# Attention of the second block: where a short block's shares stand, and the order of the last head pair's blocks

## The reference, cut to what matters

```
scale = 1 / sqrt(dqk)
sc = einsum('bqhd,bkhd->bhqk', q, k) * scale
sc = where(kpos <= qpos, sc, -inf)
o  = einsum('bhqk,bkhd->bqhd', softmax(sc), v)
```

## Time and profile before

| | us |
|---|---|
| median of 3 runs | 3968.17 (3967.4 to 3969.49) |
| the profiled execution | 3971.36 |
| its span | 3969.6 |
| TensorE busy | 3730.8 (94%) |
| VectorE busy | 2176.8 (55%) |
| ScalarE busy | 1226.5 (31%) |
| mean granted TensorE clock | 0.977 of full speed |

### The profile page before, as it was taken

One profiled execution on the slowest core, in us unless ns is written; L12 is line 12 of the kernel. 1 busy time (PEld: TensorE's weight loads), 2 busy tenths in 40 slices (PEclk: granted clock), 3 DMA queues, 4 the chain that ended last, 5 costly groups with the idle time before them and its releaser, 6 DMA issues. The chain is left out here.

```text
span 3969.6 us, 50076 instructions
## 1 busy us (share of the span) xinstructions
PE 3730.8 (94%) x19547; PEld 1925.4 (49%) x19547; DVE 2176.8 (55%) x3611; ACT 1226.5 (31%) x2432; POOL 792.3 (20%) x714
## 2 busy tenths in 40 slices
PE   6999899999899999999999989898999898998898
PEld 3444454454577774444444434344554354554443
DVE  7688426644466666533217767523555444444578
ACT  3333132465355544511110001111231254454400
POOL 0000000000566664411214332223110000000132
PEclk8999999999999999999999999999999999999999
DMA  5122664476655445401325633321111100000233
GB/s 191 48 48 52 114 133 117 113 132 120 159 179 178 170 136 171 163 32 64 117 85 180 212 108 130 106 87 61 48 38 35 34 4 6 8 4 4 72 115 111
DMA packets 594911, 385.36 MB, mean 97 GB/s; under 512 B 414468, under 2 KB 531304, under 8 KB 591988
## 3 DMA queue, kind: packets, MB, share of 16 engines
q1 hardware_dynamic: 577811, 314.52, 28.6%
q0 software_dynamic: 10336, 42.47, 3.0%
q10 hardware_dynamic: 6528, 25.17, 1.6%
HBM read 251.28 MB, written 130.55 MB: 96 GB/s over the span
## 5 line engine op out<-in xcount | busy, mean ns | idle before, releaser
L667 PE MATMUL bank<-uT,front_W 128*128 128x512 f32 (+1 forms) x1216 | 488.2, 563 | 4.7 <-ACT front_b_ L874 4.7
L599 PE MATMUL bank<-uT,front_W 128*128 128x512 f32 (+1 forms) x896 | 363.1, 563 | 0.0
L667 PEld LDWEIGHTS bank<-uT,front_W 128*128 128x128 f32 x1216 | 232.1, 192 | 252.3 <-issue 245.9
L599 PEld LDWEIGHTS bank<-uT,front_W 128*128 128x128 f32 x896 | 169.8, 191 | 182.8 <-issue 179.5
L3446 ACT ACTIVATE attn_pT<-bank 128x512 f32<-128x512 f32 x232 | 122.8, 595 | 195.5 <-PE bank L3386 194.6
L3482 DVE TENSOR_SCALAR_CACHE_REDUCE attn_sc_odd<-bank 128x512 f32<-128x512 f32 (+2 forms) x160 | 91.5, 606 | 167.1 <-PE bank L3376 167.1
L1357 POOL TENSOR_TENSOR scan_U<-scan_U,gla_w 128x512 f32<-128x512 f32 x144 | 146.9, 1041 | 168.4 <-DVE scan_U L1545 168.4
L1768 PE MATMUL bank<-gates_T,gates_S 128*128 128x512 f32 x384 | 172.7, 592 | 1.3 <-POOL uT L1730 1.3
L3373 PE MATMUL bank<-attn_kT,attn_qT 64*128 64x512 f32 (+3 forms) x640 | 151.0, 572 | 8.7 <-DVE attn_sc_odd L3482 6.3
L3398 PE MATMUL bank<-attn_pT,uT 128*64 128x256 f32 (+1 forms) x1152 | 139.2, 376 | 11.9 <-DVE attn_pT L3503 10.0
L1347 POOL TENSOR_TENSOR front_work<-front_work,eGl 128x512 f32<-128x512 f32 x144 | 146.9, 1041 | 10.6 <-DVE front_work L1564 4.3
(11 more groups left out here) (570 smaller groups left out, 7267.2 us busy)
## 6 DMA issues: line engine op xcount, KB each, us to landing
merge_gates<-gates_r ACTq DMA_DIRECT2D x16, 1024.0 KB, 4.0
uT<-merge_gates SPq DMA_DIRECT2D x16, 1024.0 KB, 10.7
gla_asks_keys_values<-front_a SPq DMA_DIRECT2D x14, 1152.0 KB, 10.8
front_W<-in_w_in SPq DMA_DIRECT2D x28, 512.0 KB, 10.6
uT<-in_w_in SPq DMA_DIRECT2D x13, 1024.0 KB, 5.3
scan_dq<-delta_qkv SPq DMA_DIRECT2D x16, 768.0 KB, 6.2
front_work<-gla_asks_keys_values SPq DMA_DIRECT2D x16, 768.0 KB, 7.0
front_work<-delta_qkv SPq DMA_DIRECT2D x16, 768.0 KB, 6.0
```

The lines of the kernel that those rows point to most:

```text
L599: m = pe.matmul(bank[:, conv_bank(f, b), 0:n], W[:, f % 2, k, :], uT[:, k, t0:t0 + n], start=(k == 0), stop=(k == KT - 1))
L667: mm = pe.matmul(bank[:, b, 0:n], W[:, s, k, :], uT[:, k, t0:t0 + n], start=(k == 0), stop=(k == KT - 1))
```

## The change

First, `rest_end(prev)` is called right behind the last group of the block before, if that block has fewer groups than this one has pieces. In pairs 1 to 3 this concerns block (a - 1, 0), whose `H` comes after the first piece and the one group instead of after the fourth piece of (a, 7). Second, the last pair takes its blocks as 7, 6, 3, 4, 1, 0, 5, 2; there the new place of `rest_end` also concerns block 3 under block 4 and block 0 under block 5. Third, the closing loop handles the groups of whatever block is last (two, for p = 2), with the product of the block before it at the first group, and changes bank pairs between groups.

```diff
-        blocks = [(a, p) for a in range(PAIRS) for p in range(TOP, -1, -1)]
+        DOWN, LAST = range(TOP, -1, -1), (7, 6, 3, 4, 1, 0, 5, 2)
+        blocks = [(a, p) for a in range(PAIRS) for p in (DOWN if a < PAIRS - 1 else LAST)]
...
                 if k < of_rest:
                     rest_items(prev, k, k >= pieces(p))
+                    if k == of_rest - 1 and of_rest < pieces(p):
+                        rest_end(prev)
...
-            if prev:
+            if prev and of_rest >= pieces(p):
                 rest_end(prev)
-        for k in range(len(groups(0))):
-            order.append(("O", *blocks[-2]))
+        for k in range(len(groups(blocks[-1][1]))):
+            if k == 0:
+                order.append(("O", *blocks[-2]))
             rest_items(blocks[-1], k, False)
+            pairs_of_banks.reverse()
         rest_end(blocks[-1])
         order.append(("O", *blocks[-1]))
```

## The result

The changed kernel takes 3987.0 us (median of 5) against 3969.5 for the kernel before (5 runs): ratio 1.0043, 95% interval 1.0028 to 1.0057, so 17.5 us slower. A second timing on another occasion gave 3985.9 against 3970.0, ratio 1.0044 (1.0031 to 1.0056). The profiled execution of the changed kernel took 3982.05 us (span 3980.3), 10.7 more than the profiled execution before; its attention is longer by 14.5 us, and it came to attention 3.8 us earlier (first scores at 3143.87 against 3147.66).

The account below looks back on a forecast made before the run. TensorE, busy for 94% of the span, was taken as the bound, with attention's end paid one for one. Moved shares 0.4, waits 9.1 and clock 6.0 sum to 15.5 us over the 3968.17 median, say 3984; range 3974 to 3992.

Parts of the forecast that it names:

- Bound and exposure: Whole kernel: TensorE is busy for 94% of the span, and the end of attention is paid one for one.
- Shares moved: Three head changes: 4.85 us of lateness goes, three delays of 1.69 come, about 0.05 remains each time; net +0.4 us.
- (a): Last pair, block 4 behind block 3: TensorE waits 3.1 us for exponentials that block 1's scores do not cover.
- (b): Last pair, block 5 behind block 0: shares wait 1.13 us, third piece 0.94, and uncovered exponentials 4.0.
- The third piece's wait: Last pair, block 5: its third piece waits 0.94 us for VectorE's evictions.
- (c): Last pair, blocks 6 and 4: two groups left to VectorE's copies add 0 us; bounds 0 and 1.
- (d): Tail of the last pair: the 1.5 us wait for VectorE's copies returns unchanged, so 0 us; bounds -1 and 0.
- The clock: Three head changes and blocks 4 and 5 of the last pair: low clock on transposes and values, 1.2 us each, 6.0.
- rival 5: The clock falls on work at all five places, 2.3 to 3.1 us each: +21 to +25 us; chance 0.16.
- Rival 1: Head changes: the shares were the true bound, lateness returns in full, last-pair waits are covered: -7.8 us, 3960.4; chance 0.05.
- rival 2: Last-pair waits about half as long, head changes give 2 us back, clock up: +2.5 to +7.5 us; chance 0.12.
- rival 3: Waits as computed, but the clock never falls on work: +9.5 us, 3977.7; chance 0.2.

Follow-up runs that it names:

- the kernel with the shares alone: Changed kernel with all four pairs in the order 7 to 0, so only the shares move at three head changes: 3977.6 us, ratio 1.0016 to the kernel before.
- the kernel with the shares moved and filled: Only the shares moved, plus 8 unread transposes ahead of and 20 behind block 6's first scores in all pairs: 3970.6 us, ratio 1.0000 to the kernel before.
- the kernel before, filled: Kernel before, plus 26 unread transposes of the identity ahead of block 0's shares in all four pairs: 3966.4 us, ratio 0.9988.
- the first two experiments: Changed kernel with only the shares moved, then with only the last pair's new order: 3977.6 and 3983.6 us, ratios 1.0016 and 1.0031 to the kernel before.
- the kernel with the late group: Kernel before, with block 0's group and shares behind block 7's last piece at three head changes, reciprocal ahead of that piece: 3970.0 us, ratio 0.9997.

## Why the prediction was right, point by point

- **Bound and exposure.** Right. The output stage is as long as before, and attention's growth is paid in full. Attention ended at 3761.37, not near 3766, because this execution came to it 3.8 us earlier.
- **Shares moved, net +0.4.** Right. The share wait was 0.97 us (1.13 forecast); the last exponential came 1.62 us later at the second head change of the kernel with the shares alone (1.69); transposes started 0.15 behind it. Lateness gone and delay added cancel: the kernel with the shares moved and filled is 0.5 us from the kernel before. That the lateness was what stuck out of the low clock, as the prediction supposed, is shown by the kernel before, filled.
- **(a) and (b), the uncovered exponentials.** Right: 3.27 and 4.24 us (3.1 and 4.0), shares 0.97 (1.13). The third piece's wait was mis-sized: it shows 1.15 (0.94), but the piece lost 2.02; the forecast read only the wait of such a piece and not what its busy rows hide. Part of (a) and (b) shows as waits for banks within the covering scores, not for ScalarE as I had said it would.
- **(c), 0.** Right: no wait for VectorE's copies was added in blocks 6 and 4.
- **(d) the tail, 0.** Mis-sized, with what stands around it. The pieces above add to 10.5, and with 0.8 of clock to 11.3; the last pair grew by 8.65. So about 2.7 us came back, and the lower bound given was -1. By the rows, 0.9 of it is in the waits for VectorE's copies, 2.7 us and 1.8 after (the 1.5 us wait came back as forecast, three short ones did not), 0.2 in a wait of transposes, and 1.6 in transposes and values that run shorter: 16 transposes take 2.04 to 2.21 us right behind scores and about 1.9 behind values or a wait, and the new order has fewer behind scores.
- **The clock, 5 x 1.2 = 6.0.** The total is near, the split was not. At the head changes it cost at least 5.9 (2.2, 2.2, 1.5 by the filled kernel), not 3.6; the low clock covered the transposes every time, for 10.2 us. In the last pair it cost 0.8, not 2.4: one stretch of 3.4 us, at block 5, and none at block 4.
- **The size.** 3984 against 3987.0 and 3985.9; attention's own +14.5 and +15.3 are closer to the sum of 15.5 than the medians are. That closeness is partly luck. The sum put 4.0 on the head changes (0.4 and 3.6 of clock) and 11.5 on the last pair (9.1 and 2.4); the trace has 6.15 and 8.65, and the two misses of 2.2 and -2.9 nearly cancel. The time lies in the band of the forecast, +11 to +20; rival 5's low clock on work held at three places of five, at about 2.2 us each. Rival 1 fell with the first two experiments and rival 2 with the waits of (a) and (b), which have their full length; rival 3 needs a clock that stays up, which happened only with added work.

On the Trainium skill's rule ("TensorE: Matmul & The Clock Gate", section Terms, penalty is half the throttled time): with 10.2 us per head change an estimate from this page is 5.1 us each. The filled kernel gives 2.2. The trace shows where the rest is: of the stretch from 3629.8 to 3640.0, all up to 3635.5 lies under block 7's exponentials, which set the time there; half of the 4.5 us behind it is 2.25. The rule gives the lost work, not the lost time.

## What to carry to other kernels

A long wait in the list is worth only the lateness of what comes after it: compare the start of the next dependent step with the end of its other input. When software-pipelined blocks differ in length, a block's latency chain (here its exponentials) must be covered by what stands behind its last piece, so a longer block after a shorter one is exposed by the difference. Where TensorE must idle just before dense work, the clock's fall is paid in the dense work. Filling the time kept the clock up here; real work moved there brought 0.6 us by itself and 2.8 us together with the fill. And a total that comes out right does not vouch for its terms: compare them stretch by stretch.

## What the runs showed of the hardware

Transposes that nobody reads, 3.06 us of them per head pair, with 8 more at the start of pair 0, took the kernel with the late group from 3970.0 to 3962.7 us (ratio to the kernel before 0.9997, then 0.9980): in attention the clock was low for 30.7 us in all without them, and never with them once the scores had begun. And the same 16 transposes took 1.9 to 2.2 us at the full granted clock and 3.67 at 0.50 of it. Ahead of such slow ones TensorE had waited 1.68 and 0.86 us around its scores (the changed kernel) or 3.69 us in one piece (group late); ahead of the fast ones of the filled kernels it had worked on the fill.
